# Expert outputs gathered and added tile by tile inside the last stage, with the gate weights loaded during the last experts

## The reference

```python
h = h + hier_moe(rmsnorm(h, norm_ffn))          # 32 experts, the best 2 of each token, FF = 256
h = h + sigmoid(rmsnorm(h, norm_ple) @ ple_gate_w) * (p @ ple_proj)
y = rmsnorm(h, norm_final)
```

## Time and profile before

| | us |
|---|---|
| median of three runs | 1907.65 |
| lowest, highest | 1900.54, 1915.2 |
| profiled execution: its own time | 1899.41 |
| profiled execution: span | 1897.6 |
| PE, DVE, ACT, POOL busy in the span | 1644.1, 665.5, 430.3, 52.4 |

### The profile page before, as it was taken

How to read it: one execution, slowest core, us unless ns; L and a number is a source line. 1 busy time by engine, 2 the same in 40 slices (tenths; PEclk the granted TensorE clock), 3 DMA queues, 4 the chain that set the end, 5 groups by cost and what they waited for, 6 DMA issues and landing times. The chain is left out here.

```text
span 1897.6 us, 35039 instructions
## 1 busy us (share of the span) xinstructions
PE 1644.1 (87%) x15296; PEld 1154.2 (61%) x15296; DVE 665.5 (35%) x1589; ACT 430.3 (23%) x864; POOL 52.4 (3%) x57
## 2 busy tenths in 40 slices
PE   3677998998997888898999988999999999980997
PEld 2355667567566565676666654555788888860443
DVE  3125555446445321524334252224311111115334
ACT  2131321421420220322313141112111111112233
POOL 0000000000000000000000000000100000004000
PEclk8878999899898788999999998999999999995999
DMA  3033031211002004424233174003799999946201
GB/s 122 14 60 25 6 23 17 32 13 16 25 2 37 19 8 177 168 112 167 113 119 161 52 281 191 34 31 147 278 371 367 363 366 368 367 159 207 116 34 39
DMA packets 61053, 246.90 MB, mean 130 GB/s; under 512 B 13024, under 2 KB 20448, under 8 KB 51168
## 3 DMA queue, kind: packets, MB, share of 16 engines
q1 hardware_dynamic: 49088, 201.61, 31.9%
q0 software_dynamic: 7200, 26.22, 3.8%
q10 hardware_dynamic: 4608, 16.78, 2.2%
HBM read 210.70 MB, written 33.88 MB: 129 GB/s over the span
## 5 line engine op out<-in xcount | busy, mean ns | idle before, releaser
L416 PE MATMUL bank<-h,w 128*128 128x352 f32 (+1 forms) x576 | 199.3, 496 | 6.3 <-DVE xb L979 6.3
L1737 PEld LDWEIGHTS bank<-cache,we 128*128 128x128 f32 x1536 | 175.1, 192 | 13.7 <-issue 10.5
L1737 PE MATMUL bank<-cache,we 128*128 128x128 f32 x1536 | 175.6, 275 | 2.8 <-DVE cache L2000 2.8
L416 PEld LDWEIGHTS bank<-h,w 128*128 128x128 f32 x576 | 109.8, 198 | 69.6 <-DVE xb L979 7.6
L2000 DVE COPY cache<-bank 128x512 f32<-128x512 f32 x64 | 41.2, 686 | 291.7 <-PE bank L1724 291.7
L1228 PE MATMUL bank<-h,w 128*128 128x352 f32 (+1 forms) x384 | 119.7, 474 | 8.3 <-POOL qd L1214 8.3
L1668 PE MATMUL bank<-cache,mixed 128*128 128x512 f32 x256 | 113.1, 601 | 2.5 <-DMA mixed<-in_i32t 2.5
L2302 PE MATMUL bank<-wp,unT 128*128 128x512 f32 x256 | 112.2, 597 | 0.0
L1228 PEld LDWEIGHTS bank<-h,w 128*128 128x128 f32 x384 | 73.6, 193 | 52.7 <-POOL qd L1214 8.9
L1749 PE MATMUL bank<-we,gated 128*128 128x512 f32 x192 | 86.4, 592 | 0.0
L1668 PEld LDWEIGHTS bank<-cache,mixed 128*128 128x128 f32 x256 | 48.9, 193 | 61.5 <-issue 59.0
(11 more groups left out here) (400 smaller groups left out, 2516.3 us busy)
## 6 DMA issues: line engine op xcount, KB each, us to landing
we<-in_weg SPq DMA_DIRECT2D x24, 1024.0 KB, 5.6
we<-in_weu SPq DMA_DIRECT2D x24, 1024.0 KB, 9.0
we<-in_wed SPq DMA_DIRECT2D x24, 1024.0 KB, 11.9
cache<-in_kcj SPq DMA_DIRECT2D x4, 5120.0 KB, 15.7
cache<-in_vcj SPq DMA_DIRECT2D x4, 5120.0 KB, 15.1
y_rows<-cache ACTq DMA_DIRECT2D x32, 512.0 KB, 8.9
cache<-in_weg SPq DMA_DIRECT2D x8, 1024.0 KB, 5.8
cache<-in_weu SPq DMA_DIRECT2D x8, 1024.0 KB, 9.2
```

The source lines that it names most:

```text
L416: mm = pe.matmul(out[:, 0:w], w3[:, KIND[q], kd, :], g.uT[:, kd, a:a + w], start=(kd == 0), stop=(kd == KD - 1))
L1737: mm = pe.matmul(bank[6 + e % 2][:, 128 * (2 * a + f):128 * (2 * a + f) + CAP], w[:, k, 128 * f:128 * f + 128], xT[e % 2][:, k, :], start= ...
```

## The change

- `feed_forward`: after the last expert's load SP waits until the down matmuls of expert 29 are done (`NE - 2` = 30 of them), and then loads the gate weights into `g.w01`, one tensor that now holds the slots 0 and 1. `rows(k)` also makes the first pass's weight and integer row indices (`g.weight`, `g.first_row`), and `g.now` is set here. `pad_a` and `position` move into the spare columns of another tensor, and `pad_a` becomes the last of `LOADS`, behind `i32t`.
- `combine` is gone as a stage. In `finish` POOL issues the same 18 gathers into four buffers, DVE adds them tile by tile ahead of each tile's norm, and each tile's 1/rms is taken by itself. TensorE's turn(1) comes after the first half of gates(0).
- `later_passes` takes its buffers from tensors that are there already, stores to a DRAM tensor of its own, and squares nothing, since `finish` now does.
- The buffers of `finish` lie in `cache`, and eight semaphores for the gate weights are cleared ahead of `feed_forward`.

```diff
 feed_forward
+        w0, w1, w3 = g.w01[:, 0:WSIZE], g.w01[:, WSIZE:2 * WSIZE], sb("we3", [128, WSIZE])
         LOADS = (...
-                 (pad_a[:, :, :], g.d_pad_a), (w4, g.d_w4), (w32, g.d_w32), (tokv[:, :], g.d_tokv), (i32t, g.d_i32t))
+                 (w4, g.d_w4), (w32, g.d_w32), (tokv[:, :], g.d_tokv), (i32t, g.d_i32t), (pad_a, g.d_pad_a))
 SP
                 for e in range(NW, NE):
                     sp.wait_ge(s["down"], e - NW + 1)
                     load_expert(sp, g, weights[e % NW], e, w_in[e % NW])
+                sp.wait_ge(s["down"], NE - 2)
+                for k in range(KD):
+                    sp.dma_start(g.wp[:, k, :], g.d_pgate[128 * k:128 * k + 128, :]).then_inc(g.wp_in[k], 16)
 DVE
+                op(dve.memset(g.now[:, :], 1.0))
 rows(k)
+                    op(dve.tensor_scalar(t2, over, 0.0, None, ALU.is_equal))
+                    op(dve.tensor_tensor(g.weight[:, k, :], t2, g.gate[:, k, :], ALU.mult))
+                    op(dve.tensor_tensor(t2, t2, g.row[:, k, :], ALU.mult))
+                    op(dve.tensor_copy(g.first_row[:, k, :], t2))
-def combine(nc, g):
...
 finish
+            @block.gpsimd
+            def _(pool):
+                for n in range(2 * TT):
+                    t, k = n // 2, n % 2
+                    if n >= 4:
+                        pool.wait_ge(combined, n - 3)
+                    pool.indirect_dma_start(y[n % 4], None, g.yb[:, :], bass.IndirectOffsetOnAxis(g.first_row[:, k, t:t + 1], 0)).then_inc(y_in[n % 4], 16)
 DVE
+                def combine(t):
+                    for k in range(2):
+                        n = 2 * t + k
+                        dve.wait_ge(y_in[n % 4], 16 * (n // 4 + 1))
+                        dve.scalar_tensor_tensor(out=g.h[:, t, :], in0=y[n % 4], scalar=g.weight[:, k, t:t + 1], in1=g.h[:, t, :],
+                                                 op0=ALU.mult, op1=ALU.add).then_inc(combined, 1)
+                        dve.drain()
                 def normalise(t):
+                    x = rstd[:, t:t + 1]
+                    dve.wait_ge(squared, t + 1)
+                    dve.tensor_scalar(x, sq[:, t:t + 1], 1.0 / D, RMS_EPS, ALU.mult, ALU.add).then_inc(meaned, 1)
+                    dve.wait_ge(rooted, t + 1)
+                    dve.reciprocal(x, x)
+                    dve.drain()
                     ...
-                dve.tensor_scalar(rstd[:, :], g.ss[:, :], 1.0 / D, RMS_EPS, ALU.mult, ALU.add).then_inc(meaned, 1)
-                dve.wait_ge(rooted, 1)
-                dve.reciprocal(rstd[:, :], rstd[:, :])
-                dve.drain()
-                normalise(0)
-                normalise(1)
+                for t in range(2):
+                    combine(t)
+                    normalise(t)
+                    turned_out(t)
                 for t in range(TT):
                     if t + 2 < TT:
+                        combine(t + 2)
                         normalise(t + 2)
+                        turned_out(t + 2)
                     ...
 PE
                 turn(0)
-                turn(1)
                 ...
+                            if t == 0 and i == 0:
+                                turn(1)
 ACT
+                def square(t):
+                    act.wait_ge(combined, 2 * t + 2)
+                    act.activation(junk, g.h[:, t, :], ACT.Square, accum_out=sq[:, t:t + 1]).then_inc(squared, 1)
+                    act.wait_ge(meaned, t + 1)
+                    act.activation(rstd[:, t:t + 1], rstd[:, t:t + 1], ACT.Sqrt).then_inc(rooted, 1)
+                square(0)
+                square(1)
                 for t in range(TT):
+                    if t + 2 < TT:
+                        square(t + 2)
                     act.wait_ge(gates, t + 1)
                     ...
```

More of the change, by code:

```diff
@@ L1562, in feed_forward @@
         wo = g.wo
-        w0, w1, w3 = (sb(f"we{i}", [128, WSIZE]) for i in (0, 1, 3))
-        weights = g.weights = [split_weights(x) for x in (w0[:, :], w1[:, :], g.cache[:, 0:WSIZE], w3[:, :])]
+        w0, w1, w3 = g.w01[:, 0:WSIZE], g.w01[:, WSIZE:2 * WSIZE], sb("we3", [128, WSIZE])
+        weights = [split_weights(x) for x in (w0, w1, g.cache[:, 0:WSIZE], w3[:, :])]
         gain, junk = w1[:, 0:D], w1[:, D:2 * D]
@@ L1594, in feed_forward @@
         valid, tokv = sb("valid", [128, TT]), sb("tokv", [128, TT])
-        pad_a, position = sb("pad_a", [128, 2, TT]), sb("position", [128, 2, TT])
+        position, pad_a = (g.spare[:, a:a + 2 * TT].rearrange("p (k t) -> p k t", k=2) for a in (480, 500))
         idx = g.idx = sb("idx", [128, NE], i32)
@@ L2067, in later_passes @@
         bank = g.bank
-        weights = [split_weights(sb(f"lw{i}", [128, WSIZE])[:, :]) for i in range(2)]
+        weights = [split_weights(x) for x in (g.cache[:, 0:WSIZE], sb("lw1", [128, WSIZE])[:, :])]
         idx, tok = sb("l_idx", [128, NE], i32), sb("l_tok", [128, TT], i32)
-        xg, yo, junk = sb("l_xg", [128, D]), sb("l_yo", [128, D]), sb("l_junk", [128, D])
-        y = [sb(f"l_y{i}", [128, D]) for i in range(2)]
-        xT, silu, hT = sb("l_xT", [128, KD, CAP]), sb("l_silu", [128, 2, CAP]), sb("l_hT", [128, 2, CAP])
+        xg, y = g.w3[:, 0:D], [g.w3[:, D * (i + 1):D * (i + 2)] for i in range(2)]
+        yo, xT = g.cache[:, 6 * D:7 * D], g.cache[:, 7 * D:8 * D].rearrange("p (k q) -> p k q", k=KD)
+        silu, hT = (g.cache[:, 8 * D + 256 * i:8 * D + 256 * i + 256].rearrange("p (f q) -> p f q", f=2) for i in range(2))
         now, here = g.now, sb("l_here", [128, 2, TT])
@@ L2186, in _ @@
                         dve.wait_ge(s[f"y{n % 2}"], p * (16 * TT) - 16 * (TT - n // 2 - 1))
-                        dve.scalar_tensor_tensor(out=g.h[:, t, :], in0=y[n % 2][:, :], scalar=weight[:, k, t:t + 1], in1=g.h[:, t, :],
+                        dve.scalar_tensor_tensor(out=g.h[:, t, :], in0=y[n % 2], scalar=weight[:, k, t:t + 1], in1=g.h[:, t, :],
                                                  op0=ALU.mult, op1=ALU.add).then_inc(s["combined"], 1)
                         dve.drain()
[L2191 to L2196, removed]
                 @block.gpsimd
@@ L2217, in finish @@
         bank = g.bank
[L2218 to L2224, removed]
+        wp = g.wp
+        y = [g.cache[:, i * D:i * D + D] for i in range(4)]
+        fgain, junk = g.cache[:, 4 * D:5 * D], g.cache[:, 5 * D:6 * D]
+        un, sig = (g.cache[:, a * D:(a + 2) * D].rearrange("p (i d) -> p i d", i=2) for a in (6, 8))
+        uT = sb("unT", [128, 2, KD, 128])
+        rstd, ss, sq, rout = (sb(n, [128, TT]) for n in ("frstd", "fss", "fsq", "frout"))
+        names = "gain_in combined squared meaned rooted normed turned evac gates sigd updated y_squared y_meaned y_rooted y_ready outs"
+        gain_in, combined, squared, meaned, rooted, normed, turned, evac, gates, sigd, updated, y_squared, y_meaned, y_rooted, y_ready, outs = (
             sem("f_" + n) for n in names.split())
+        y_in = [sem(f"f_y{i}") for i in range(4)]
         c = PC["norm_ple"]
@@ L2230, in _ @@
             def _(sp):
-                for k in range(KD):
-                    sp.dma_start(wp[:, k, :], g.d_pgate[128 * k:128 * k + 128, :]).then_inc(w_in[k], 16)
-                sp.dma_start(fgain[:, :], g.d_final_gain).then_inc(gain_in, 16)
+                sp.dma_start(fgain, g.d_final_gain).then_inc(gain_in, 16)
                 for t in range(TT):
@@ L2324, in _ @@
                     act.wait_ge(updated, t + 1)
-                    act.activation(junk[0:r, :], g.h[0:r, t, :], ACT.Square, accum_out=ss[0:r, t:t + 1]).then_inc(squared, 1)
+                    act.activation(junk[0:r, :], g.h[0:r, t, :], ACT.Square, accum_out=ss[0:r, t:t + 1]).then_inc(y_squared, 1)
                     act.wait_ge(y_meaned, t + 1)
@@ L2448, in build @@
         g.yb = nc.dram_tensor("y_rows", (NE * CAP, D), f32, kind="Internal").ap()
+        g.yb2 = nc.dram_tensor("y_rows_later", (NE * CAP, D), f32, kind="Internal").ap()
         g.h = sb("h", [128, TT, D])
@@ L2486, in build @@
             g.row, g.turn = sm("row", [128, 2, TT]), sm("turn", [128, 2, TT])
+            g.weight, g.first_row = sm("weight", [128, 2, TT]), sm("first_row", [128, 2, TT], i32)
+            g.w01 = sm("we01", [128, 2 * WSIZE])
+            g.wp = g.w01[:, 0:KD * D].rearrange("p (k d) -> p k d", k=KD)
+            g.wp_in = [mix.enter_context(nc.semaphore(f"wp_in{k}")) for k in range(KD)]
+            g.new += g.wp_in
             feed_forward(nc, g)
-            combine(nc, g)
             later_passes(nc, g)
```

18 lines of the change are left out of this document (8 added, 10 removed).

## The result

| | before | after |
|---|---|---|
| runs beside each other, median (lowest to highest) | 1906.29 (1900.54 to 1915.2) | 1876.05 (1875.07 to 1877.41) |
| time of the profiled execution | 1899.41 | 1875.94 |
| span of the profile | 1897.6 | 1874.1 |

The ratio is 0.9841, 95% interval 0.9808 to 0.9874: 30 us or 1.6% faster. The forecast was 1875.5 us and a gain of 30.2.

What follows compares the result with a forecast made beforehand. Experts and last stage were taken as bound by TensorE, with a 53.6 us pause between. -40.5 + 7.3 + 0.9 (turn(1) inside gates(0)) + 1.2 + 0.6 + 0.3 = -30.2 us, from 1905.7 to 1875.5; range 1863 to 1886.

Steps and rivals of the forecast that it cites:

- Forty us for the stage that went: Between experts and `finish`: without `combine` all that follows starts 40.5 us earlier, the way from clears to entry staying 6.3.
- 7.3 us at the start: Entry of `finish` to first gates: gathers, additions, gain, norm and turn(0) take 15.9 us, 7.3 more than 8.6.
- The clock: First gates of `finish`: more work at 1.2 GHz costs +1.2 us over the 0.98 before, bounds 0 to +3.
- The weights: Gate weights loaded beside the last experts: issued about 1688, landed about 1702, costing TensorE nothing.
- The steady part: Tiles of `finish`: the chain with additions takes 14.18 us against TensorE's 14.60, so nothing is lost, margin 0.42.
- Clears and `pad_a`: Ahead of and at the start of `feed_forward`: eight more clears cost +0.6 us, `pad_a` landing last costs +0.3.
- The level: Whole program: the gain is taken from 1905.7 us, the mean of all four runs, not from the profiled 1899.41.
- (a): Steady part of `finish`: one more table load, 1.28 us, makes the chain 15.5 us; total 1881; chance 0.06.
- (b): Steady part of `finish`: POOL's 0.98 us loss falls on DVE at both gathers, 1.6 per tile; total 1885; chance 0.03.
- (c): Start of `finish`: branch, gathers, clock and store all at upper bounds, 8 us; total about 1884; chance 0.06.
- (d): Start of `finish`: late weights, or waits of first gathers and gates, cost 15 us or more; 1890 to 1900; chance 0.07.
- (e): `finish`: late `un` makes TensorE pause and its clock fall to 1.2 GHz; +27 us, 1932 us; chance 0.04.

Runs made afterwards that it cites:

- no_branch: The changed kernel without the branch over the later passes and without their code; 1875.43 us, ratio to before 0.9849.
- clears_hidden: The changed kernel with semaphores of later passes and last stage cleared by POOL inside `feed_forward`, without the two later clearing blocks; 1868.35 us, ratio to before 0.9803.
- gain_late: The changed kernel, but the final gain's load waits until the first tile is added; 1872.27 us, ratio to before 0.9808.
- combine_alone: The changed kernel, but with the gate weights loaded at the start of `finish` as before; 1876.2 us, ratio to before 0.9838.
- un_twice: The changed kernel with the instruction that writes `un` given twice per tile; 1880.63 us, ratio to before 0.9863.
- un_five: The changed kernel with the instruction that writes `un` given five times per tile; 1901.59 us, ratio to before 0.9967.

## Why the prediction was right

**Forty us for the stage that went.** The step was: what follows starts 40.5 us earlier, since the way through clears and branch stays 6.3. With the changed kernel's late start, 7.7 us, taken off, entry is at 1712.1 where 1712.5 was said. TensorE's branch took 3.57 us after a short idle time, and 3.69 and 3.39 in the two profiles of before, after a long one. That this branch was last is shown by no_branch (entry 2.95 us sooner without it) and clears_hidden (4.9 us sooner once the others need not wait for it).

**7.3 us at the start: 0.6 too few.** From entry to gates 16.56 us, predicted 15.9. The added 0.65 are GpSimd's between entry and its first gather, which I had at nothing. The rest held by term: second addition 7.49 after the first gather (6.38 + 1.0), then 3.78 (3.8) and 3.36 (3.4). The 1.0 for the gain was in part luck: 7.49 is one draw out of 6.62 to 8.21, and gain_late and the others put the gain's own share nearer to 0.4.

**The clock.** The first half of gates(0) took 8.79 against 6.87, a loss of 1.92; 0.98 + 1.2 were predicted. This term varied most: 8.66 to 10.18 for that half over the ten profiles in which TensorE comes to it at 1.2 GHz. A profile at the upper end would have put it 1.1 us over the forecast, well inside the bounds.

**The weights.** Issued from 1695.3 to 1699.1, landed up to 11.1 us after (by 1710.2, about 1702 in the time of the first profile), and the last store was issued at 1710.48. TensorE had no gap beside them (busy for 33.33 us of 33.33). But what they are worth is 2.6 us, by combine_alone, and nothing without the other half. The sum had no such term and needed none, as both halves were made at once.

**The steady part.** Chain 14.18 predicted; by un_twice it is 14.36 once TensorE waits, and 0.46 us of margin while it doesn't (0.42 was said). From turn(1) to turn(2) the margin is 0.28, 1752.86 against `un` written at 1752.58 (0.3 was said). Beyond the margin the period is the chain's, as un_twice and un_five show with 15.19 and 17.7 us; the price named for it was 0.6 per tile for 1 us more, and un_twice paid 0.58 for 0.83, a little more than that. The tail after the last gates took 18.96 us (18.99 before), unchanged as said. GpSimd's slow issues (1.92) lay on GpSimd alone.

**What the page's drain would have made.** The Trainium skill's ScalarE: Activation LUTs, What ACT_TABLE_LOAD costs, has a drain of about 1.38 us with each switch of tables. In the start-up of the changed kernel the load began 0.02 us after the square's end (1730.39 - 1730.37) and the root 0.02 us after the load's end (1731.69 - 1731.67), so the trace doesn't agree, and the sum was right to leave it out.

**Clears and `pad_a`.** 0.6 and 0.3 predicted. The eight clears cost 0.6 (TensorE idle for 7.56 us ahead of `feed_forward`, 6.99 before). `pad_a` cost 0.07: TensorE waited 2.56 us for it and 2.49 for `i32t`. The changed kernel's rows:

```profile
1150.02 3.85 PE L1760 MATMUL bank<-ones,mixed 128*128 128x1 f32 x18 [7.56 <-PEq L2421]
1156.43 3.89 PE L1673 MATMUL bank<-cache,mixed 128*128 128x512 f32 x5 [2.56 <-DMA mixed<-in_pad_a]
```

**The level.** The choice of 1905.7 in place of the profiled 1899.41 decided the absolute number: medians of before were 1904 to 1910 in four comparisons. The mechanism is confirmed term by term, but that the total fell within 0.6 us is luck: the terms missed by up to 0.65 us, some up and some down, and the medians of the two comparisons give gains of 30.2 and 32.1 us.

Rivals (a) and (b) are excluded by the profile, (c) by the start's terms. (d) and (e) did not come; un_five gave (e) the long chain that it asked for, and the time was 1901.59 us and not 1932.

## What to carry to other kernels

A stage that is bound by one engine is room: count the other engines' chain per tile, including what one tile hands to the next, and work with less than the remainder is free. Two loads or two stages that hide in the same room are worth different amounts alone and together; take each away once before crediting it. A block boundary makes all engines wait for the slowest thing between, here one engine's branch, so a boundary removed can be worth more than the instructions in it.

## What the runs showed of the hardware

- The taken branch over the later passes took TensorE 3.39 to 3.89 us in all thirteen profiles that have it, and the other engines 0.05 to 0.08 us in the changed kernel. The Trainium skill, Runtime: NRT & Kernel Launch, Instruction fetch mechanics, says that a taken branch whose target isn't in the fetched window stalls for a fetch; that fits, and doesn't say why it was TensorE alone.
- Pauses of 0.4 us left TensorE's clock at 2.4 GHz, with a granted clock of 1.00 over the tiles of un_twice; with pauses of 3 us, in un_five, it was 0.90 to 0.92 in three of six tiles and 0.99 to 1.00 in the others. In either case, where the clock was 2.4 GHz, the eight transposes after a pause took 0.24 us more than those it ran into (1.11 and 0.87).
- The same DMA engines moved 364 GB/s in the experts' stage (weights, gathers and stores mixed, share 0.97) and 410 to 418 GB/s in combine_alone while gate weights and gathers were read.
- Beside the two additions of a tile one issue of a gather took GpSimd 1.92 us in place of 0.94, and the additions kept their 2.65 us for both.
